# A depthwise convolution of 31 taps in a hybrid decoder layer: how its taps are shared among VectorE, ScalarE and GpSimd

## What is computed

```python
u = rmsnorm(h, norm_g)
p = u @ w_in          # q|k|v (12 tiles of 128), z (4), beta|alpha, GLU value and gate (4 + 4)
q, k, v = split(silu(causal_dwconv(qkv_ext, qkv_conv_w)))     # 4 taps
o = gated_delta_chunked(q, k, v, g, beta, state, 64)          # then norm, times silu(z)
c_in = val * sigmoid(gate)                                    # 512 channels
c_ext = concatenate([s_conv, c_in], axis=1)                   # 30 rows of history
c = causal_dwconv(c_ext, conv_w) + conv_b                     # 31 taps: what the change moves
c = silu(rmsnorm(c, conv_norm_g))
h = h + concatenate([o, c], axis=-1) @ w_out
```

## Time and profile before

| | |
|---|---|
| median of 3 runs | 1404.17 us |
| lowest, highest | 1402.92, 1406.08 us |
| profiled execution: span from the first to the last instruction | 1402.5 us |
| profiled execution: own time | the page gives none outside its span |
| PE busy | 1293.9 us (92%) |
| DVE busy | 686.6 us (49%) |
| ACT busy | 461.4 us (33%) |
| POOL busy | 264.7 us (19%), 184 instructions |
| mean granted clock of PE | 0.951 of full |

### The profile page before, as it was taken

The page is one execution under the profiler, slowest core; times in us unless marked ns, Lnnn a source line. Parts: engine busy times, 40 slices in busy tenths (PEclk is TensorE's granted clock), DMA queues, the critical chain, the costliest instruction groups (busy, mean ns, idle before and its releaser), DMA issues.

```text
span 1402.5 us, 22544 instructions
## 1 busy us (share of the span) xinstructions
PE 1293.9 (92%) x9129; PEld 1259.3 (90%) x9129; DVE 686.6 (49%) x817; ACT 461.4 (33%) x703; POOL 264.7 (19%) x184
## 2 busy tenths in 40 slices
PE   5999999999999999886668898999999999999995
PEld 5999999999999899885567886799999999999995
DVE  5543334433447348884788653634443344333443
ACT  5432122211224565556333323424331122212232
POOL 3000000000003465445863422220000000000011
PEclk9999999999999999997778996799999999999998
DMA  6222222222223131110000000321222222222252
GB/s 206 91 81 84 78 84 79 75 90 76 75 90 105 61 121 60 60 61 16 1 1 1 1 1 15 132 87 53 91 81 80 84 76 75 90 75 77 89 92 74
DMA packets 35831, 100.52 MB, mean 72 GB/s; under 512 B 11840, under 2 KB 12224, under 8 KB 35392
## 3 DMA queue, kind: packets, MB, share of 16 engines
q1 hardware_dynamic: 35632, 97.40, 22.0%
q10 hardware_dynamic: 144, 2.36, 0.5%
HBM read 94.24 MB, written 5.50 MB: 71 GB/s over the span
## 4 chain that ended last, share of the span: by engine, by line
PE 76%; DVE 14%; issue 4%; ACT 3%; POOL 2%; DMA 0%; POOLq 0%; DVEq 0%; ACTq 0%; SPq 0%
PE ps L359 67%; PE ps L435 8%; DVE work L1180 4%; DVE work L1205 2%; POOL work L1478 2%; DVE work L1178 1%; ACT w_hi L714 1%; DVE x_lo L1044 1%; DVE d_inv_t L1307 1%; DVE d_inv L1304 1%; PE ps L410 0%; DMA raw<-weights 0%; DVE d_decay L1245 0%; DVE h L1432 0%; DVE w_lo L1039 0%
## 5 line engine op out<-in xcount | busy, mean ns | idle before, releaser
L359 PE MATMUL ps<-x_hi,w_hi 128*128 128x296 f32 x1920 | 425.0, 303 | 31.3 <-DVE x_lo L1044 19.6
L359 PE MATMUL ps<-x_hi,w_lo 128*128 128x296 f32 x1920 | 421.7, 301 | 0.0
L359 PE MATMUL ps<-x_lo,w_hi 128*128 128x296 f32 x1920 | 421.0, 301 | 0.0
L359 PEld LDWEIGHTS ps<-x_hi,w_hi 128*128 128x128 f32 x1920 | 315.2, 191 | 35.7 <-issue 22.6
L359 PEld LDWEIGHTS ps<-x_lo,w_hi 128*128 128x128 f32 x1920 | 316.0, 191 | 0.0
L359 PEld LDWEIGHTS ps<-x_hi,w_lo 128*128 128x128 f32 x1920 | 314.7, 190 | 0.0
L1039 DVE TENSOR_TENSOR w_lo<-raw,w_hi 128x1024 fp32r<-128x1024 f32 x168 | 208.3, 1241 | 205.9 <-ACT w_hi L714 203.8
L714 ACT CAST w_hi<-raw 128x1024 fp32r<-128x1024 f32 x168 | 174.7, 1041 | 262.2 <-PE ps L359 236.2
L1451 POOL COPY ssum<-sq 128x592 f32<-128x592 f32 x4 | 4.5, 1134 | 834.4 <-ACT sq L720 834.4
L359 PE MATMUL ps<-g_hi,w_hi 128*128 128x296 f32 x704 | 153.6, 299 | 1.0 <-DVE g_lo L1069 1.0
L359 PE MATMUL ps<-g_hi,w_lo 128*128 128x296 f32 x704 | 153.4, 299 | 0.0
(11 more groups left out here) (199 smaller groups left out, 1198.8 us busy)
## 6 DMA issues: line engine op xcount, KB each, us to landing
raw<-weights SPq DMA_DIRECT2D x168, 512.0 KB, 3.3
h<-x_t SPq DMA_DIRECT2D x2, 1184.0 KB, 5.5
y_t<-h SPq DMA_DIRECT2D x8, 296.0 KB, 2.4
new_state<-S ACTq DMA_DIRECT2D x1, 2304.0 KB, 8.3
S<-states SPq DMA_DIRECT2D x1, 2048.0 KB, 10.6
mask<-masks SPq DMA_DIRECT2D x1, 836.5 KB, 7.8
c_ext<-hist_c SPq DMA_DIRECT2D x4, 120.0 KB, 8.2
last_c<-c_ext SPq DMA_DIRECT2D x4, 120.0 KB, 9.1
```

What stands on the lines that cost most here:

```text
L359: last = nc.tensor.matmul(ps[:, slot, half, 0:HALF], w[:, slot, k, :], x[:, k, half * HALF:(half + 1) * HALF], start=(k == 0 and n == 0), ...
```

## The change

Three of the four channel tiles, 1 to 3, are now done by DVE as fused multiply-adds (93 taps, lines 1136 to 1149 of the changed kernel), in two instructions each, prompt and sample. Tile 0 stays with ACT and POOL (30 products and additions, and POOL's first tap). DVE's taps stand in other places: 5 after each weight split of the GLU tiles c = 2 and 3 (20), 2 within each q/k/v unit behind its first multiplication (24), 7 behind each z scaling (28), and one behind each level (21, with which all are done). ACT does its 30 products four at a time, two times per GLU tile from c = 1 on (24), and the last six in the first two q/k/v units. The `taps` steps of the schedule are gone. POOL adds its 30 right after another, ahead of the delta stage. ACT waits for the sums of tiles 1 to 3 on two semaphores of DVE, one for the prompt parts and one for the sample parts. No DMA is added, removed or moved.

```diff
-POOL_TAPS = 3 * (CW - 1)
-EARLY_TAPS = 8 * 3 + 3 * NQ + H
+TAPS = NC_ * CW
+POOL_TAPS = CW - 1
+GLU_TAPS, QKV_TAPS, Z_TAPS, LEVEL_TAPS = 5, 2, 7, 1
...
-    taps = [("taps", 0, i) for i in range((POOL_TAPS - EARLY_TAPS + 1) // 2)]
-    out = [("gates", 0, i) for i in range(3)] + merge(merge(prep[0], prep[1]), taps[0:4])
+    out = [("gates", 0, i) for i in range(3)] + merge(prep[0], prep[1])
...
-    out += merge(merge(merge(chain[0], chain[1][:lag1]), tok[0] + tok[1] + prep[2]), taps[4:])
+    out += merge(merge(chain[0], chain[1][:lag1]), tok[0] + tok[1] + prep[2])
...
 # ScalarE, GLU tiles
                 if c:
-                    conv_taps(8)
+                    conv_taps(4)
...
                 split_hi(u + 5, (u + 5) % 4)
+                if c:
+                    conv_taps(4)
...
 # ScalarE, z units
-                conv_taps(1)
...
 # VectorE
+            def conv_taps(n):
+
+                for t in range(taps[0], min(taps[0] + n, TAPS - CW)):
+                    c, j = 1 + t // CW, t % CW
+                    out = work[:, 4 + c, 0:L]
+                    x = c_ext[:, c, j:j + L]
+                    if j == 0:
+                        dve.wait_ge(c_in_ready, c + 1)
+                        V.tensor_scalar(out, x, v("conv_w", CW * c), v("conv_b", c), ALU.mult,
+                                        ALU.add).then_inc(conv_prompt, 1)
+                    else:
+                        dve.wait_ge(conv_prompt, t)
+                        V.scalar_tensor_tensor(out, x, v("conv_w", CW * c + j), out, ALU.mult,
+                                               ALU.add).then_inc(conv_prompt, 1)
+                    out = work[:, 4 + c, L:TOK].rearrange("p (b w) -> p b w", b=NB)
...
                 split_lo(u + 4, (u + 4) % 4)
+                if c > 1:
+                    conv_taps(GLU_TAPS)
...
                 split_lo(u + 5, (u + 5) % 4)
+                if c > 1:
+                    conv_taps(GLU_TAPS)
...
                 link(V.tensor_scalar(a[:, 0:QO], e[:, 0:QO], v("qkv_conv_w", SC * i), None, ALU.mult))
+                conv_taps(QKV_TAPS)
...
                 scaled(z[:, i, :], u, u % 4).then_inc(psum_free, 1)
+                conv_taps(Z_TAPS)
...
-                    conv_taps(2 if t < 2 else 1)
+                    conv_taps(LEVEL_TAPS)
...
 # GpSimd
-            conv_taps(0, EARLY_TAPS)
+            for t in range(POOL_TAPS):
+                pool.wait_ge(tap_ready, t + 1)
+                if t:
+                    pool.wait_ge(tap_added, t)
+                G.tensor_tensor(out[:, 0:TOK], out[:, 0:TOK], tap_place(t)[:, 0:TOK], ALU.add).then_inc(tap_added, 1)
```

More of the change, by code:

```diff
@@ L668, in _ @@
             steps = {"gates": gates, "prep": prep, "tok": tok, "start": start, "level": level, "end": end, "scan": scan,
-                     "conv": conv, "samples": samples, "final": final, "weights": weights_split, "taps": taps_step}
+                     "conv": conv, "samples": samples, "final": final, "weights": weights_split}
             for name, t, i in delta_schedule():
@@ L789, in conv_taps @@
                 for t in range(taps[0], min(taps[0] + n, POOL_TAPS)):
[L790 to L791 removed]
+                    j = 1 + t
+                    act.wait_ge(c_in_ready, 1)
                     if t >= 3:
@@ L1130, in gate_inputs @@
                 V.scalar_tensor_tensor(gate["t1"][:], gate["g"][:], -1.0, gate["g"][:], ALU.mult, ALU.max).then_inc(ab_ready, 1)
+            taps = [0]
+            def conv_taps(n):
[12 more added lines that the diff above has]
+                    out = work[:, 4 + c, L:TOK].rearrange("p (b w) -> p b w", b=NB)
+                    x = c_ext[:, c, CP:CE].rearrange("p (b w) -> p b w", b=NB)[:, :, j:j + LB]
+                    if j == 0:
+                        V.tensor_scalar(out, x, v("conv_w", CW * c), v("conv_b", c), ALU.mult,
+                                        ALU.add).then_inc(conv_sample, 1)
+                    else:
+                        dve.wait_ge(conv_sample, t)
+                        V.scalar_tensor_tensor(out, x, v("conv_w", CW * c + j), out, ALU.mult,
+                                               ALU.add).then_inc(conv_sample, 1)
+                taps[0] = min(taps[0] + n, TAPS - CW)
             for c in range(NC_):
@@ L1190, in _ @@
                 scaled(z[:, i, :], u, u % 4).then_inc(psum_free, 1)
-            taps = [0]
-            def conv_taps(n):
-                out, c = work[:, 7, :], 3
-                parts = ((out[:, 0:L], lambda j: c_ext[:, c, j:j + L]),
-                         (out[:, L:TOK].rearrange("p (b w) -> p b w", b=NB),
-                          lambda j: c_ext[:, c, CP:CE].rearrange("p (b w) -> p b w", b=NB)[:, :, j:j + LB]))
-                for j in range(taps[0], min(taps[0] + n, CW)):
-                    if j:
-                        dve.wait_ge(conv3_step, j)
-                    for o, x in parts:
-                        if j:
-                            last = V.scalar_tensor_tensor(o, x(j), v("conv_w", CW * c + j), o, ALU.mult, ALU.add)
-                        else:
-                            last = V.tensor_scalar(o, x(j), v("conv_w", CW * c), v("conv_b", c), ALU.mult, ALU.add)
-                    last.then_inc(conv3_step, 1)
-                taps[0] += n
+                conv_taps(Z_TAPS)
             def gates(_, i):
@@ L1346, in conv @@
                 if c == 0:
-                    conv_taps(CW)
+                    conv_taps(TAPS)
                 if c == 4:
```

43 lines of the change are left out of this document (12 added, 31 removed).

## The result

| | before | after |
|---|---|---|
| median | 1404.13 us (1398.16 to 1406.08, 10 runs) | 1410.39 us (1405.75 to 1415.93, 10 runs) |
| ratio, 95% interval | | 1.0048 (1.0031 to 1.0065) |
| span of the profiled execution | 1402.5 us | 1406.2 us |
| DVE / ACT / POOL busy | 686.6 / 461.4 / 264.7 us | 714.6 / 409.7 / 181.3 us |

The change makes the kernel slower by 0.5%; 1410.0 was forecast. Less lies behind this agreement than it seems: two prices were wrong, with opposite signs.

The account below looks back on a forecast made before the run. DVE was taken to bound the q/k/v stage and to be nearly full in the delta stage's first part. +30.6 up to the gate-sum copy less 24.8 in the delta stage gave +5.8, 1410.0 us; range 1396 to 1422.

Parts of the forecast that it names:

- A tap, 0.98 us: Price on DVE of one tap, a 528-wide and a 64-wide instruction, where no addition is near: 0.98 us.
- An addition, 0.90 us: What one GpSimd addition costs DVE where DVE is full: 0.90 us, read from a q/k/v unit.
- Rival 3: An addition costs DVE its whole duration, 1.23 us, for 24 additions: +13.7 in all, 1417.9 us; chance 0.09.
- Full DVE: From 500 to 680 us, GLU to z stage, DVE has no gap over 2 us in the new profile.
- TensorE's stand costs nothing: z stage: TensorE stands still some 20 us before its gate products, costed at nothing because its granted clock is low already.
- (a): Delta stage, from the copy of the gate sums up to the first level: 4.8 us come back, bounds 1.7 and 7.
- first two items: Before the first level: two products leave ScalarE's chain, 1.7 us; two DVE steps lose their additions, 1.7 us.
- (b): Delta stage, 690 to 746 us: fewer taps free 19.9 us of DVE, 15 come back; bounds 8 and 20.
- (c): Delta stage, 746 to 806 us: fewer taps free 9.5 us of DVE, 5 come back; bounds 3 and 9.
- Rival 1: DVE stays the delta stage's bound and gives back all it is relieved of: -5.4, 1398.8 us, faster; chance 0.24.
- rival 2: TensorE's own chain of levels replaces the taps in the delta stage, 15.8 come back: +14.8, 1419.0 us; chance 0.12.
- Rival 4: Few GLU-stage taps meet an addition and idle time swallows them, so the halves cancel: about 1404 us; chance 0.05.

Follow-up runs that it names:

- one_semaphore: The changed kernel with the wait scheme of the kernel before: only a tap's 64-wide instruction waits and signals, on one semaphore; 1414.6 us, 1.0087 of the kernel before.
- warm_pe: The changed kernel with 18 unread 512-column products more on TensorE, where it stands still before the gate products; 1409.2 us, 1.0041 of the kernel before.
- z_last28: The changed kernel with the four z scalings together and all 28 z-stage taps behind them, ahead of the gate-sum copy; 1409.4 us, 1.0033 of the kernel before.
- before_split: The kernel before with ScalarE's eight products per GLU tile done four and four instead of eight together; 1403.4 us, 0.999 of the kernel before.

## Why the prediction was right, and where it was only lucky

- **The sign and the size** hold: +5.8 forecast on the span, +3.7 measured there (+5.2 from the scaling on) and +6.2 in the medians. The mechanism is the forecast's: the front loses more (+26.7, or +28.3) than the delta stage returns (-23.0). Up to the first q/k/v unit 22.6 us are lost, the q/k/v units give 8.6 of them back, and the z stage loses 14.3 more.
- **A tap, 0.98 us: mis-sized.** It is 0.88 (653.50 - 652.62). That is why the z scalings lie 6.81 and not 7.5 us apart and the z stage took 27.0 (677.23 - 650.19) and not 30.0, and why the q/k/v units took 7.93 and not 8.2. The row was of the same operation and shape, but with other waits around it; one_semaphore brings 1.00 back, and 4.2 us with it.
- **An addition, 0.90 us: mis-sized**, some 1.2. Rival 3's mechanism is right in the place where it matters, and I had given it 0.09. The error was hidden, and that is luck: the additions took 28.3 us up to the copy and not 24 x 0.90 = 21.6, which makes +7, and the 72 taps at 0.10 us less make -7. The count of 21 additions that meet DVE in the GLU stage (measured: 20) was good. That stage took +22.6 and not +19.1: the additions +6 (24.8 and not 18.9), the taps -2. In the q/k/v and z stages the forecast was 6 us too long, 5 of them by its 52 taps.
- **Where the 0.90 came from.** It is no average that hides the price. In the kernel before, each of the two fused multiply-adds that meet an addition in a unit like that of the earlier trace rows takes 1.72 us instead of 0.86. This is the first one of the unit ahead of it:

```profile
588.83 1.72 DVE L1180 SCALAR_TENSOR_TENSOR work<-work,vec 128x616 f32<-128x616 f32 x1
```

  There each instruction waits for the one before it, and from start to start of two it is 1.75 us with an addition and 0.89 without. In the unit at 541.94 of the same trace the same four instructions take 1.75 + 5.22 us, so the price was not one number even there. Why a tap of two instructions pays 2.09 - 0.88 = 1.21 and a chained one 0.86 isn't shown. The Trainium skill (SBUF — State Buffer, "SBUF: two separate sides") states that a DVE instruction with two inputs in SBUF and a GpSimd instruction that reads SBUF lock each other out for a whole instruction. The 64-wide instruction held for 1.48 us and the addition stretched from 1.23 to 1.94 agree; in the q/k/v units the measured price is less than the whole 1.23, and there the measurement decides.
- **Full DVE** in front: right. The largest gaps are the 1.70 us for `w_hi`. The forecast had the row that shows such a wait, and did not see that taps ahead of a split fill it at no cost.
- **TensorE's stand costs nothing:** right within what the runs can tell, though warm_pe and z_last28 had to show it. The waits of TensorE, POOL and ACT in the z stage were 19.8, 103.6 and 18.1 us long, and ending them earlier gained nothing.
- **(a), 4.8 us: mis-sized**, 1.4, and only 0.2 against before_split, whose code there is that of the kernel before (37.2). Up to the first level's first product the gain is 3.2 us (33.79 to 30.62 us behind the copy), near the 1.7 + 1.7 of the first two items; the estimated 1.4 for mask and subtract steps did not come, and TensorE's lower clock took 1.8 back in the level itself. The forecast had put the clock's price at the stand, where it is nothing, and not here.
- **(b) and (c)**, -15 and -5: -16.3 and -5.3. The sizes came as forecast; that part of what DVE freed becomes waiting for TensorE is the forecast's argument, and no run takes it apart. Rival 1 (all comes back) and rival 2 (11 of it) both fail by 7 us or more.
- Rival 4 (few additions meet DVE's work in the GLU stage, so the halves cancel) fails: 20 did.

## What to carry to other kernels

Before work is put on an engine as cover, ask whose copy stands behind it in that engine's queue: a tap of 0.88 us cost 0.75 ahead of one small copy and 0.4 to 0.5 between the steps of a chain, and a tap ahead of a wait that was there anyway cost nothing. A price taken from a row holds with the waits and neighbours of that row, so compare those with the diff's before using it: both the tap and the addition were priced right for their own place and wrong for the new one. And when two profiles are compared, look for the last instruction ahead of the first changed one; here 1.5 us of the difference lay before it. Where two engines shut each other out, the third of the additions that was left still cost some 30 us.

## What the runs showed of the hardware

- An instruction of 64 elements a partition on DVE, 0.28 us alone, took 1.48 beside a GpSimd addition, and it did not matter that it is small: the two engines take turns, one tap to an addition, 2.09 us a turn. A chained 616-wide fused multiply-add, 0.86 alone, took 1.72. Even a 24-wide copy took 1.35 to 1.39 us instead of 0.18. The evacuations that read PSUM (0.46 us for 296 columns) were not stretched beside additions in before_split (0.45).
- A wait for the instruction just before on DVE costs 0.12 us more than one for the instruction before that (0.32 against 0.20 from start to start of the next).
- 15.6 us of products that ended 43 us before the second product of the first level left TensorE's clock there at its lower level (granted 0.50, 2.08 us for eight products); 5.5 us of them in the waits right before brought it to the higher (granted 1.00, 1.16 us).
